# Recurrent heads of a two-layer decoder step: four coarser level products in one visit of TensorE, and both transposes in one visit

## What is computed

```python
def gla_chunked(q, k, v, log_f, S0):
    ...
    def step(S, inp):
        qc, kc, vc, lc = inp
        G = jnp.cumsum(lc, axis=2)
        diff = G[:, :, :, None, :] - G[:, :, None, :, :]
        decay = jnp.exp(jnp.where(causal[:, :, None], diff, -jnp.inf))
        A = jnp.einsum('bhtd,bhsd,bhtsd->bhts', qc, kc, decay)
        o = jnp.einsum('bhts,bhse->bhte', A, vc) + jnp.einsum('bhtd,bhde->bhte', qc * jnp.exp(G), S)
        Gl = G[:, :, -1]
        S = jnp.exp(Gl)[..., None] * S + jnp.einsum('bhsd,bhse->bhde', kc * jnp.exp(Gl[:, :, None] - G), vc)
        return S, o

def mixer_c(xn, S0, w_in, lb, norm_g, w_out):
    q, f, i, g = jnp.split(xn @ w_in, [C_DK_T, 2 * C_DK_T, 2 * C_DK_T + C_DV_T], axis=-1)
    ...
    o = rms_norm(o, norm_g).reshape(Bsz, L, C_DV_T) * jax.nn.silu(g.astype(f32))
    return o.astype(xn.dtype) @ w_out, S.astype(S0.dtype)
```

## Time and profile before

| | us |
|---|---|
| median of 3 runs (1358.7 to 1358.9) | 1358.71 |
| the profiled execution | 1358.26 |
| its span, first to last instruction | 1356.5 |
| busy in the span: TensorE / VectorE / ScalarE / GpSimd | 1323.3 / 817.7 / 602.5 / 233.6 |
| one pass of the recurrent stage, 716.00 to 749.47 | 33.47 |
| in that pass busy: TensorE / VectorE / ScalarE / GpSimd | 33.07 / 28.88 / 22.72 / 9.61 |
| mean granted TensorE clock | 0.994 of 2.4 GHz |

### The profile page before, as it was taken

How to read it: one execution, slowest core, us unless ns; L and a number is a source line. 1 busy time by engine, 2 the same in 40 slices (tenths; PEclk the granted TensorE clock), 3 DMA queues, 4 the chain that set the end, 5 groups by cost and what they waited for, 6 DMA issues and landing times.

```text
span 1356.5 us, 30303 instructions
## 1 busy us (share of the span) xinstructions
PE 1323.3 (98%) x11820; PEld 1290.5 (95%) x11820; DVE 817.7 (60%) x1401; ACT 602.5 (44%) x1230; POOL 233.6 (17%) x365
## 2 busy tenths in 40 slices
PE   8999999999999999997999999999999999999997
PEld 8998999999999999996999999989999999999996
DVE  6476576656565622248888888867566555552224
ACT  5366355433333322236666666655533333332221
POOL 3111121111111100001322222211111111120000
PEclk9999999999999999999999999999999999999999
DMA  7311231323222332213323232322122222332211
GB/s 272 116 60 63 81 94 48 94 89 93 89 81 91 108 104 89 74 49 92 111 95 95 95 95 95 95 96 94 40 94 85 87 83 93 99 119 87 86 43 66
DMA packets 39683, 123.39 MB, mean 91 GB/s; under 512 B 4232, under 2 KB 12040, under 8 KB 39496
## 3 DMA queue, kind: packets, MB, share of 16 engines
q1 hardware_dynamic: 35400, 111.92, 26.1%
q10 hardware_dynamic: 4048, 10.20, 2.2%
q0 software_dynamic: 176, 0.44, 0.1%
HBM read 113.98 MB, written 8.57 MB: 90 GB/s over the span
## 4 chain that ended last, share of the span: by engine, by line
PE 78%; DVE 10%; ACT 5%; issue 4%; POOL 1%; DMA 0%; ACTq 0%; DVEq 0%; SPq 0%; POOLq 0%
PE acc L428 74%; DVE w_lo L1310 1%; ACT w_hi L846 1%; DVE lev L1661 1%; DVE x L1516 1%; ACT Snew L1262 1%; DVE mix L1511 1%; DVE Snew L1792 1%; DVE scratch L1778 1%; DVE AT L1728 1%; PE aux L587 0%; DVE lev L1667 0%; ACT AT L1224 0%; DMA x<-in_xT 0%; DVE h_lo L1319 0%
## 5 line engine op out<-in xcount | busy, mean ns | idle before, releaser
L1310 DVE TENSOR_TENSOR w_lo<-raw,w_hi 128x512 fp32r<-128x512 f32 (+1 forms) x372 | 306.4, 827 | 335.0 <-ACT w_hi L846 334.6
L428 PE MATMUL acc<-h_hi,w_hi 128*128 128x272 f32 x2208 | 477.2, 294 | 7.1 <-DVE w_lo L1310 2.3
L428 PE MATMUL acc<-h_hi,w_lo 128*128 128x272 f32 x2208 | 465.3, 289 | 0.0
L428 PE MATMUL acc<-h_lo,w_hi 128*128 128x272 f32 x2208 | 464.0, 288 | 0.0
L428 PEld LDWEIGHTS acc<-h_hi,w_hi 128*128 128x128 f32 x2208 | 350.7, 189 | 18.4 <-issue 7.4
L846 ACT CAST w_hi<-raw 128x512 fp32r<-128x512 f32 (+1 forms) x372 | 236.5, 642 | 267.2 <-PE acc L428 262.2
L428 PEld LDWEIGHTS acc<-h_lo,w_hi 128*128 128x128 f32 x2208 | 350.8, 189 | 0.2
L428 PEld LDWEIGHTS acc<-h_hi,w_lo 128*128 128x128 f32 x2208 | 348.7, 189 | 0.0
L428 PE MATMUL acc<-g_hi,w_hi 128*128 128x272 f32 x704 | 153.1, 288 | 0.0
L428 PE MATMUL acc<-g_hi,w_lo 128*128 128x272 f32 x704 | 153.0, 289 | 0.0
L428 PE MATMUL acc<-g_lo,w_hi 128*128 128x272 f32 x704 | 152.4, 288 | 0.0
(11 more groups left out here) (247 smaller groups left out, 1418.8 us busy)
## 6 DMA issues: line engine op xcount, KB each, us to landing
raw<-in_w_up SPq DMA_DIRECT2D x88, 512.0 KB, 3.5
raw<-in_w_down SPq DMA_DIRECT2D x32, 704.0 KB, 4.1
raw<-in_w_in_c SPq DMA_DIRECT2D x32, 512.0 KB, 3.6
raw<-in_w_in_ab SPq DMA_DIRECT2D x18, 512.0 KB, 3.7
raw<-in_w_out_ab SPq DMA_DIRECT2D x8, 512.0 KB, 3.5
S<-in_state ACTq DMA_DIRECT2D x8, 512.0 KB, 3.6
o_ss<-Snew ACTq DMA_DIRECT2D x8, 512.0 KB, 2.7
raw<-in_w_out_c SPq DMA_DIRECT2D x8, 512.0 KB, 3.5
```

Source lines behind the costliest of these rows:

```text
L428: mm = pe.matmul(acc[out][:, t, 0:H], w[slot][:, wc], mv[:, kk_, t * H:(t + 1) * H], start=start and k == 0 and q == 0, stop=stop and k == ...
L1310: dve.tensor_tensor(w_lo[slot][:, to], raw[n % 4][:, cols], w_hi[slot][:, to], ALU.subtract).then_inc(lo_ready, 1)
```

## The change

In the recurrent stage TensorE does all four coarser level products at tick 2, and nothing at tick 1; and it does the key transposes at tick 6, ahead of the value transposes, in every pass. ScalarE does the six copies to `AT` at tick 2, behind Ln, and the three copies of the transposed key at tick 6. VectorE folds levels 3 and 4 into `AT` between the step that ends the forget gate (L1806) and the wait for Ln, when there is a `cur`, where it did so ahead of the `c_kk` steps; it waits for `lev_ready` ahead of `c_kk`; and it does `kdT_lo` at tick 6, behind `level_q(1)`. Instructions, shapes and buffers stay as they were.

```diff
--- before.py
+++ after.py
@@ -733,15 +733,12 @@
                         for c in range(NCH):
                             mm = pe.matmul(A[0][:, c * P:(c + 1) * P], kt[:, c, :], vt[:, c, :], start=True, stop=True)
                         mm.then_inc(C["u_done"], 1)
-                    if t == 1:
+                    if t == 2:
                         pe.wait_ge(C["lev_ready"], 8 * prev + 8)
                         pe.wait_ge(C["al_taken"], 4 * prev + 2)
-                        levels(prev, 1)
-                        levels(prev, 2)
-                    if t == 2:
                         pe.wait_ge(C["st_ready"], prev + 1)
-                        levels(prev, 3)
-                        levels(prev, 4)
+                        for which in range(1, 5):
+                            levels(prev, which)
                     if t == 3:
                         pe.wait_ge(C["al_copied"], prev + 1)
                         pe.wait_ge(C["al_taken"], 4 * prev + 4)
@@ -773,7 +770,7 @@
                                   ).then_inc(C["ostat_done"], 1)
                 if cur is not None:

-                    if t == (6 if prev is None else 5):
+                    if t == 6:
                         pe.wait_ge(C["kd_ready"], cur + 1)
                         if prev is not None:
                             pe.wait_ge(C["ors_ready"], prev + 1)
@@ -1211,7 +1208,11 @@
                         step.mark(act.activation(S[1][:], S[0][:], ACT.Ln, bias=1.0))
                         step.wait(act)
                         act.activation(S[1][:], S[1][:], ACT.Exp, scale=-1.0).then_inc(C["sig_ready"], 1)
-                if prev is not None and t == 1:
+                if cur is not None:
+                    if t == 2:
+                        act.wait_ge(C["ff_ready"], cur + 1)
+                        act.activation(S[1][:], S[1][:], ACT.Ln).then_inc(C["lf_ready"], 1)
+                if prev is not None and t == 2:
                     wide_, narrow = [z[:, 0:s].rearrange("p (c s) -> p c s", c=2) for z, s in ((A[2], 128), (A[3], 64))]
                     pairs = AT[:].rearrange("p (c r t) -> p r c t", c=2, r=2)
                     act.wait_ge(C["al_taken"], 4 * prev + 2)
@@ -1225,19 +1226,11 @@
                                           narrow[32 * (2 * n + z):32 * (2 * n + z) + 32])
                     i_.then_inc(C["al_copied"], 1)
                 if cur is not None:
-                    if t == 2:
-                        act.wait_ge(C["ff_ready"], cur + 1)
-                        act.activation(S[1][:], S[1][:], ACT.Ln).then_inc(C["lf_ready"], 1)
                     if t == 3:
                         act.wait_ge(C["G_ready"], cur + 1)
                         act.activation(eG[:], G[:], ACT.Exp).then_inc(C["eG_ready"], 1)
                         act.wait_ge(C["kd_diff"], cur + 1)
                         act.activation(kd[:], kd[:], ACT.Exp).then_inc(C["kd_exp"], 1)
-                    if t == 5:
-                        act.wait_ge(C["kdT_done"], cur + 1)
-                        act.copy(kt[:].rearrange("p a b -> p (a b)"), A[0][:])
-                        act.copy(kt_s[R1, :], A[1][R0, 0:P])
-                        act.copy(kt_s[R0, :], A[1][R0, 0:P]).then_inc(C["kdT_hi"], 1)
                 if prev is not None and t == 5:
                     act.wait_ge(C["oy_ready"], prev + 1)
                     act.copy(y_hi[:, prev, :], S[3][:]).then_inc(C["oy_hi"], 1)
@@ -1262,6 +1255,10 @@
                             i_ = act.activation(Snew[:, b, :], S0[:, b, :], ACT.Copy, scale=eG[:, last:last + 1])
                         i_.then_inc(C["s0_scaled"], 1)
                     if t == 6:
+                        act.wait_ge(C["kdT_done"], cur + 1)
+                        act.copy(kt[:].rearrange("p a b -> p (a b)"), A[0][:])
+                        act.copy(kt_s[R1, :], A[1][R0, 0:P])
+                        act.copy(kt_s[R0, :], A[1][R0, 0:P]).then_inc(C["kdT_hi"], 1)
                         act.wait_ge(C["vcT_done"], cur + 1)
                         act.copy(vt[:].rearrange("p a b -> p (a b)"), A[3][:])
                         act.copy(vt_s[:], A[2][R0, 0:P]).then_inc(C["vcT_copied"], 1)
@@ -1761,7 +1758,7 @@
                         dve.wait_ge(C["v_lo"], prev + 1)
                         v3 = v3_s[:].rearrange("p (a b) -> p a b", a=1).broadcast_to([3 * NB * TS, NB, P])
                         dve.tensor_tensor(vbd[:], v3, own[:], ALU.mult).then_inc(C["vbd_ready"], 1)
-                    if t == 2:
+                    if t == 2 and cur is None:
                         take_level(prev, 3)
                         take_level(prev, 4)
                     if t == 4:
@@ -1778,7 +1775,6 @@
                         dve.tensor_tensor(S[3][:], S[3][:], sg[:], ALU.mult).then_inc(C["oy_ready"], 1)
                         if cur is not None:
                             level_ops(2, cur)
-                            kdT_lo(cur)
                         dve.wait_ge(C["oy_hi"], prev + 1)
                         dve.tensor_tensor(y_lo[:, prev, :], S[3][:], y_hi[:, prev, :], ALU.subtract
                                           ).then_inc(C["oy_lo"], 1)
@@ -1800,6 +1796,8 @@

                     one_lb = lb[:, 7, cur:cur + 1] if isinstance(cur, int) else lb[:, 7, bass.ds(cur, 1)]
                     low = lb[:, 6, cur:cur + 1] if isinstance(cur, int) else lb[:, 6, bass.ds(cur, 1)]
+                    if prev is not None:
+                        dve.wait_ge(C["lev_ready"], 8 * prev + 8)
                     dve.scalar_tensor_tensor(kk[:], S[0][:], one_lb, S[1][:], ALU.mult, ALU.mult)
                     step.mark(dve.tensor_scalar(S[1][:], S[1][:], one_lb, low, ALU.mult, ALU.add))
                     step.wait(dve)
@@ -1807,6 +1805,9 @@
                     if prev is None:
                         dve.wait_ge(const_c, 64)
                         dve.wait_ge(set_up, 5)
+                    else:
+                        take_level(prev, 3)
+                        take_level(prev, 4)
                     dve.wait_ge(C["lf_ready"], cur + 1)
                     dve.tensor_tensor_scan(G[:], keep[:], S[1][:], 0.0, ALU.mult, ALU.add).then_inc(C["G_ready"], 1)
                 if prev is None and t == 3:
@@ -1818,14 +1819,13 @@
                 if t == 5:
                     if prev is None:
                         level_ops(2, cur)
-                    if prev is None:
-                        kdT_lo(cur)
                     level_q(0, cur)
                     dve.wait_ge(C["diag_exp"], cur + 1)
                     dve.tensor_tensor(E2[:], E2[:], kk[:], ALU.mult).then_inc(C["diag_ready"], 1)
                 if t == 6:
                     level_ops(3, cur)
                     level_q(1, cur)
+                    kdT_lo(cur)
                     dve.wait_ge(C["v_hi"], cur + 1)
                     dve.tensor_tensor(v3_s[R1, :], vt_s[:], v_hi_s[:], ALU.subtract).then_inc(C["v_lo"], 1)
                 if t == 7:
```

## The result

| | before | after |
|---|---|---|
| median, us | 1358.7 (4 runs, 1357.7 to 1358.9) | **1385.26** (4 runs, 1383.1 to 1388.8) |
| the profiled execution, its span | 1358.26, 1356.5 | 1386.58, 1384.5 |
| L771 (after: L768), first and seventh pass | 668.42, 869.05 | 670.99, 896.67 |
| mean granted clock | 0.994 | 0.982 |

The ratio is 1.0196, 95% interval 1.0184 to 1.0208: 26.6 us slower. The forecast was 1374.5 with a range to 1381. The direction was right, the size was not: +15.8 forecast, +26.6 measured, 4.3 us above the range.

The account below looks back on a forecast made before the run. The prediction took a closed ring of ScalarE and VectorE work with one TensorE visit as the bound. The profiled 1358.26 plus 11.3 gave 1369.6, the median 1370.0, and 4.5 for the clock 1374.5 us, range 1367 to 1381.

Parts of the forecast that it names:

- The ring: Recurrent stage: a closed loop of ScalarE and VectorE work with one TensorE visit sets the pass, 33.44 us.
- TensorE's slack: TensorE waits about 0.7 us per pass, 0.30 at tick 3 and about 0.42 at tick 4; shortening its stream buys nothing.
- the two merges: Two fewer TensorE visits per pass save 0.3 us, bounds 0 and 0.4, worth nothing to the span.
- Part 2, the order: Ticks 1 and 2: scan unmoved from the sigmoid chain, AT complete at 730.7 instead of 728.4, new TensorE stall at tick 3.
- Part 3, what is late next: Tick 3 to norm sums: a TensorE stretch of 6.35 us replaces 4.46 on VectorE in the ring, +1.89 per pass.
- Part 4, kdT_lo: Moving transposes and kdT_lo to tick 6 gains 0.25 us per pass, bounds -0.32 and +0.3; nearly nothing if level_q(0) meets GpSimd.
- the 0.05 at the scan: VectorE's scan of G at tick 2 comes slightly earlier, taking 0.05 us off each pass.
- Sum without the clock: Recurrent stage: +1.6 us per pass, six passes 9.6, first pass +1.75, together +11.3; bounds 1.3 and 2.1 per pass.
- Part 5, the last tick 0: After the last pass kdT_lo's later place may delay tick 0; taken as 0, bounds 0 and 1.5 us.
- The clock: TensorE's idling at tick 3 halves its clock in three of six later passes, 1.5 us each, +4.5.
- falls in nearly each pass, or longer: Rival: the clock falls in nearly each later pass, or for longer than 3.4 us: 1379 to 1388, chance 0.12.
- The faster rival: Tick 2: copies no longer ahead of the cast, so c_kk begins 2.3 us earlier and TensorE's waits vanish: 1352, chance 0.03.

Follow-up runs that it names:

- transposes_only: The kernel before with only the key transposes, their ScalarE copies and kdT_lo moved to tick 6: 1360.03 us for 1358.86, ratio 1.0006.
- both_first: The changed kernel with the six AT copies ahead of Ln and the fold-ins ahead of c_kk, all visits merged: 1355.78 us, ratio 0.9978.
- cast_first: The kernel before, no visit merged, with the six AT copies at tick 2 behind its cast and ahead of Ln: 1355.61 us, ratio 0.9974.
- warm8: The changed kernel with 8 idle matmuls of ones (fillers) in TensorE's stall before tick 3: 1372.38 us for 1358.88.
- warm12: The changed kernel with 12 idle matmuls of ones (fillers) in TensorE's stall before tick 3: 1374.05 us for 1358.89.
- copies_first: The changed kernel with the six AT copies ahead of Ln, fold-ins still behind the forget gate: 1358.32 us for 1358.86, ratio 0.9995.
- warm4: The changed kernel with 4 idle matmuls of ones (fillers) at the head of TensorE's stall before tick 3: 1386.84 us for 1358.88.
- short_transposes: transposes_only with GpSimd's key multiplies of levels 1 and 2 cut to the first 4 columns per block: 1356.97 us for 1358.5.
- levels_only: The changed kernel with the key transposes, their copies and kdT_lo back at tick 5: 1388.62 us for 1358.86, ratio 1.022.
- warm: The changed kernel with 18 idle matmuls of ones (fillers) before TensorE's tick 3 wait: 1380.4 us for 1358.86.

## Why the prediction was right and wrong, step by step

- **The ring, and TensorE's slack** (right). Merging alone was worth nothing in time (`transposes_only`, and `both_first` against `cast_first`). The 0.3 per pass taken for the two merges is near the 0.26 in the traces of those two, which goes into TensorE's wait for Snew.
- **Part 2, the order** (right). Scan 8.0 behind the sigmoid chain, AT complete at the scan instead of 2.3 ahead of it, stall at L747 (2.83 to 2.90 idle in the later passes, where some 2.4 was forecast).
- **Part 3, what is late next** (right). Tick 3 to norm sums 6.29 to 6.38 at full clock for the 6.35 taken. With eight fillers the pass takes 35.35, +1.91 per pass; the forecast was +1.6.
- **Part 4, kdT_lo** (wrong size). Taken as -0.25 per pass, measured nothing. The doubt was written down, with the row of level_q(0); the collision came one instruction earlier, on y_lo. It and the 0.05 at the scan, which did not come either, are the 0.3 per pass between 1.6 and 1.91, 1.8 us in six passes. Sum without the clock: 11.3 forecast, 13.5 measured (`warm8`). The bounds per pass of that sum, 1.3 and 2.1, don't follow from its own terms, which give 1.80 - 0.32 - 0.05 = 1.43 and 2.05 + 0.30 - 0.05 = 2.30; the 1.91 lies inside both.
- **Part 5, the last tick 0** (wrong size, by a missing consequence). Its delay was bounded by 1.5 and put at 0. Without a fallen clock it costs 0.4 (28.59 for 28.23, in the changed kernel and in `warm12`); in four other runs TensorE's 2.6 idle cost the clock, and the stage 1.3 to 1.5 us.
- **The clock** (the step that failed). The mechanism was named, and its place in the ring. The term was mis-sized: 4.5 forecast, 13 measured. It has two factors: *how many*, three of six taken, six of six measured, because the stall was placed by eye between a harmless 1.59 and a harmful 4.26; the row that should have weighed more is the 1.78 at 10.05. And *how much each*, 1.5 taken, 1.5 and 2.9 measured: the price came from one stretch of 3.4 us, though the window at 638 to 643 in the earlier trace rows already showed a longer one, which was left to a rival with a chance of 0.12. That rival ("falls in nearly each pass, or longer") is what happened, and its 1379 to 1388 holds the time.
- **The faster rival** named its own condition (copies ahead of Ln, end by 726.8) and the runs bear it out. It put the end of the copies 4.0 behind the start of the sigmoid chain (726.8 - 722.79); `copies_first` (724.05 to 727.89) and `both_first` (723.65 to 727.49) have 3.84, and TensorE's idle time at tick 3 shrinks to 0.6 and to nothing. The price given for it, 1352, was too good by 4 to 6 us: in `both_first` Snew still holds tick 4, in `copies_first` the fold-ins still hold tick 3.

Open: why the half clock lasts about 3.5 us in one pass and 6.9 in the next (from the grants: 2 x 0.22 x 7.88 and 2 x 0.37 x 9.27), and whether the merged visits are worth anything once the order is right.

## To carry to other kernels

An engine that is 98% busy may still not be the bound: look whether its few small waits are released by the same instruction in each pass, and follow that instruction back until the chain meets itself. Merging visits moves results to the later of two places; before doing it, list for each result who waits for it and what stands ahead of its copy in the copying engine's queue. And price a new TensorE stall of about 2 us or more on a critical stretch with the half clock behind it, not with its own length.

## What the hardware showed that was not expected

- An idle piece of 2.83 to 2.90 us of TensorE cost the clock in six later passes of six, and one of 1.94 to 1.99 in five of six (`warm4`); but 1.98 in the first pass of the changed kernel did not. 1.02 to 1.10 cost it in none (`warm8`), and the one piece of 1.59 or 1.60 behind the stage in no profile. One of 1.72 did, in the last tick 0 of `short_transposes` (mean grant 0.54 from 880.5 to 884.2). So the length of the piece alone does not decide.
- A fall costs 1.5 or 2.9 us in the 6.35 us behind it, in turn from pass to pass in the changed kernel, not in turn in `levels_only` (9.28, 7.95, 7.90, 9.25, 7.93, 9.25). Of the last tick 0's waits of 2.6, all alike, four cost the clock (`transposes_only`, `copies_first`, `both_first`, `warm`) and four did not (the changed kernel, `warm4`, `warm8`, `warm12`).
- Sixteen instructions of idle work on ones in each pass, 1.95 us long, made the whole changed kernel 12.9 us faster.
